# Dots with the experts of the last 14 first keys as one dense product of all prompt tokens, in a decoder step with product-key experts

## The reference, cut to what matters

```python
q = einsum('nd,de->ne', xf, w_q).reshape(N, 8, 2, 128)          # 8 heads, two half queries
sc = einsum('nhpc,pkc->nhpk', q, sub_keys)                      # 128 first keys, 128 second keys
s_top, i_top = top_k(sc, 16)
c_top, c_idx = top_k(all 256 sums of a first and a second, 16)
experts = e1 * 128 + e2                                         # 8 x 16 = 128 experts a token
gates = softmax(c_top)
h = einsum('nd,nkd->nk', xt, u_tab[experts])                    # dots with gathered rows of u
a = gates * gelu(h)
y = einsum('nk,nkd->nd', a, v_tab[experts])
```

## Time and profile before

| | us |
|---|---|
| median of 3 runs | 2494.46 (2492.43 to 2494.79) |
| profiled execution, its own time | 2485.81 |
| its span, first to last instruction | 2483.7 |
| PE busy | 1895.3 (76%) |
| DVE busy | 1708.6 (69%) |
| POOL busy | 1109.0 (45%) |
| ACT busy | 976.6 (39%) |
| mean transfer rate | 356 GB/s |

### The profile page before, as it was taken

The page is one execution under the profiler, slowest core; times in us unless marked ns, Lnnn a source line. Parts: engine busy times, 40 slices in busy tenths (PEclk is TensorE's granted clock), DMA queues, the critical chain, the costliest instruction groups (busy, mean ns, idle before and its releaser), DMA issues.

```text
span 2483.7 us, 27261 instructions
## 1 busy us (share of the span) xinstructions
PE 1895.3 (76%) x10395; PEld 1566.3 (63%) x10395; DVE 1708.6 (69%) x2335; ACT 976.6 (39%) x1603; POOL 1109.0 (45%) x484
## 2 busy tenths in 40 slices
PE   6998899899979745344233331999999999999798
PEld 5875778788769625343133231777777777777676
DVE  1056232422157988878899999899898988987723
ACT  3223122223223211111399992544444444444332
POOL 3663233345536346777676886122221222221154
PEclk9998899999989977667655555999999999999899
DMA  9997999988889879999999999899998999998547
GB/s 342 381 391 271 374 420 416 410 352 313 321 315 362 293 289 395 376 421 421 421 371 388 422 417 385 322 391 380 378 371 336 370 352 379 357 371 296 211 186 262
DMA packets 131808, 883.58 MB, mean 356 GB/s; under 512 B 19010, under 2 KB 20610, under 8 KB 55588
## 3 DMA queue, kind: packets, MB, share of 16 engines
q1 hardware_dynamic: 76388, 479.23, 50.7%
q0 software_dynamic: 55296, 402.68, 40.6%
HBM read 871.28 MB, written 141.63 MB: 408 GB/s over the span
## 4 chain that ended last, share of the span: by engine, by line
issue 28%; PE 25%; DMA 17%; DVE 14%; POOL 13%; ACT 2%; POOLq 0%; SPq 0%; ACTq 0%; DVEq 0%
DMA v_raw<-in_peer_v 9%; PE psum L1544 7%; PE psum L1546 7%; PE psum L1545 7%; POOL w_lo L553 6%; DMA expert_rows<-in_peer_u,experts 6%; POOL expert_rows L583 6%; DVE expert_rows L1355 5%; DVE v_lo L1486 2%; DVE x_tokens L1430 2%; DVE expert_rows L1421 2%; DMA ansposed_expert_rows<-in_peer_u,experts 1%; ACT v_hi L896 1%; PE psum L1891 1%; DMA ple_tokens<-in_p_sample 1%
## 5 line engine op out<-in xcount | busy, mean ns | idle before, releaser
L553 POOL TENSOR_TENSOR w_lo<-w_raw,w_hi 128x2048 fp32r<-128x2048 f32 x80 | 374.5, 4682 | 458.1 <-ACT w_hi L614 458.1
L583 POOL DMA_INDIRECT expert_rows<-in_peer_u,experts x238 | 466.1, 1958 | 186.8 <-DVE expert_rows L1355 117.1
L1544 PE MATMUL psum<-v_hi,gate_matrix_hi 128*128 128x512 f32 x1024 | 406.9, 397 | 38.9 <-DVE v_lo L1486 38.6
L896 ACT ACTIVATE v_hi<-v_raw 128x1024 fp32r<-128x1024 f32 x256 | 271.4, 1061 | 408.3 <-DMA v_raw<-in_peer_v 320.1
L1355 DVE SCALAR_TENSOR_TENSOR expert_rows<-expert_rows,x_tokens 128x2048 f32<-128x2048 f32 x174 | 393.4, 2289 | 45.6 <-DMA expert_rows<-in_peer_u,experts 43.3
L1545 PE MATMUL psum<-v_lo,gate_matrix_hi 128*128 128x512 f32 x1024 | 400.2, 391 | 0.0
L1546 PE MATMUL psum<-v_hi,gate_matrix_lo 128*128 128x512 f32 x1024 | 400.1, 391 | 0.0
L1486 DVE TENSOR_TENSOR v_lo<-v_raw,v_hi 128x1024 fp32r<-128x1024 f32 x256 | 310.1, 1220 | 85.0 <-ACT v_hi L896 84.4
L614 ACT ACTIVATE w_hi<-w_raw 128x2048 fp32r<-128x2048 f32 x80 | 153.2, 1915 | 374.4 <-PE psum L1546 285.0
L1544 PEld LDWEIGHTS psum<-v_hi,gate_matrix_hi 128*128 128x128 f32 x1024 | 192.8, 188 | 104.9 <-issue 40.2
L1846 PE MATMUL psum<-one_hot_first_gated,one_hot_second 128*128 128x128 f32 x448 | 107.7, 417 | 170.7 <-ACT one_hot_first_gated L800 167.5
(11 more groups left out here) (339 smaller groups left out, 3523.4 us busy)
## 6 DMA issues: line engine op xcount, KB each, us to landing
v_raw<-in_peer_v SPq DMA_DIRECT2D x256, 512.0 KB, 7.3
out<-in_state_attn_k SPq DMA_DIRECT2D x64, 1020.0 KB, 10.9
out<-in_state_attn_v SPq DMA_DIRECT2D x64, 1020.0 KB, 10.5
w_raw<-in_w_in SPq DMA_DIRECT2D x48, 1024.0 KB, 8.4
cache_part<-in_k_parts SPq DMA_DIRECT2D x40, 1024.0 KB, 10.5
cache_part<-in_v_parts SPq DMA_DIRECT2D x40, 1024.0 KB, 13.0
w_raw<-in_w_out SPq DMA_DIRECT2D x16, 1024.0 KB, 7.2
w_raw<-in_peer_wq SPq DMA_DIRECT2D x16, 1024.0 KB, 6.1
```

The lines of the kernel that those rows point to most:

```text
L553: nc.gpsimd.tensor_tensor(l_, r_, h_.bitcast(f32), ALU.subtract).then_inc(w_lo_ready, 1)
L583: pool.indirect_dma_start(ring[slot_of(n)][:, :], None, u_tab, bass.IndirectOffsetOnAxis(idx_p[:, t - 1, j:j + 1], 0)).then_inc(u_in[slot_ ...
L896: A(vhi[m % HS][:, :], vrl[m % RL][:, :], ACT.Copy).then_inc(vh_ok, 1)
L1544: MM(out, lh, rh, start=start, stop=False)
```

## The change

- `peer_u_T` is a further input: for each of the 14 first keys 114 to 127 the block of 128 rows of `u`, transposed to [128, 16, 128] (1 MB), laid out on the host.
- SP loads these blocks to two slots (`ut`) once the embedding output is written; PE multiplies each with all 256 prompt tokens (`block_product`: 16 products of 128 x 128 by 256 columns), block i - 1 behind PE row i. ACT applies gelu (`gelu_product`), and SP writes the results, [128 second keys, 14, 256 tokens], to the tensor `gelu_tab` in DRAM, in two parts behind the last load.
- `tokT` holds both halves' tokens. Their transposes (eight quarters, the second half's in pieces of 64 rows from two tiles) and copies stand behind the embedding product.
- The prompt's gathers get `bounds_check=KEPT`: a row index above 128 x 114 - 1 isn't gathered, and the slot keeps what it held. Three slots are zeroed once by POOL (three memsets, behind `lows(0, 66)`).
- `clear_dense` sets the dots of such pairs to 0, and `weigh` adds 1 to the gelu of 0, so that `gm` holds the plain gate there (`dense_pairs` makes the two masks).
- In the v stage, for k from 114, SP loads `gelu_tab[:, k]` (128 KB) to one of three slots ahead of piece 2k; DVE multiplies it by `gm[:, :, k]` behind piece 2k - 3 (`gate_times_gelu`), and the high and low parts are made from the product.
- `pe_dot(i)` stands behind the vector row with j = 6i + 10 (at most 109) of the first half's list.
- The builds wait for the gelus: ACT for `h_out`, PE for `h_ok`.

The diff, cut to its core:

```diff
+KD, KS = 14, 8
+K0 = NK - KD
+KEPT = K0 * 128 - 1
+PE_DOT_AT = {min(6 * i + 10, 109): i for i in range(len(PE_ROWS))}
...
+            sp.wait_ge(ple_out, 32)
+            for i in range(KD):
+                if i >= 2:
+                    sp.wait_ge(hd_mm, i - 1)
+                sp.dma_start(ut[i % 2][:, :, :].rearrange("p c s -> p (c s)"), peer_u_T[i]).then_inc(ut_in[i % 2], 16)
+            sp.wait_ge(h_ok, KS)
+            sp.dma_start(gelu_tab[:, 0:KS, :], gelu_a[:, :, :]).then_inc(h_out, 16)
+            sp.wait_ge(h_ok, KD)
+            sp.dma_start(gelu_tab[:, KS:KD, :], gelu_b[:, :, :]).then_inc(h_out, 16)
...
                 if m >= RL:
                     sp.wait_ge(vd_used, m - RL + 1)
+                if m == 2 * K0:
+                    sp.wait_ge(h_out, 32)
+                if m % 2 == 0 and m >= 2 * K0:
+                    i = m // 2 - K0
+                    if i >= 3:
+                        sp.wait_ge(al_ok, K0 + i - 2)
+                    sp.dma_start(gbuf[:, i % 3, :], gelu_tab[:, i, :]).then_inc(gk_in[i % 3], 16)
                 sp.dma_start(vrl[m % RL][:, :], v_rows[:, m // 2, m % 2, :]).then_inc(v_raw[m % RL], 16)
...
-            lows(0, 80)
+            lows(0, 66)
+            pool.wait_ge(w_used, 64)
+            for i in range(DSLOT, NSLOT):
+                nc.gpsimd.memset(ring[i][:, :], 0.0).then_inc(ring_set, 1)
+            lows(66, 14)
...
                 pool.indirect_dma_start(ring[slot_of(n)][:, :], None, u_tab,
-                                        bass.IndirectOffsetOnAxis(idx_p[:, t - 1, j:j + 1], 0)).then_inc(u_in[slot_of(n)], 16)
+                                        bass.IndirectOffsetOnAxis(idx_p[:, t - 1, j:j + 1], 0),
+                                        bounds_check=KEPT, oob_is_err=False).then_inc(u_in[slot_of(n)], 16)
...
+            def gelu_product(i):
+                if i == 0:
+                    act.wait_ge(ple_out, 32)
+                act.wait_ge(hd_mm, i + 1)
+                A(gelu_a[:, i, :] if i < KS else gelu_b[:, i - KS, :], PS[:, 6 + i % 2, 0:256], ACT.Gelu).then_inc(h_ok, 1)
...
-            act.wait_ge(ple_out, 32)
+            act.wait_ge(h_out, 32)
             one_hots(0)
...
-                    A(ghs[:, k % ST, :], gm[:, :, k], ACT.Copy).then_inc(ah_ok, 1)
+                    if k >= K0:
+                        act.wait_ge(gk_ok, k - K0 + 1)
+                    A(ghs[:, k % ST, :], weights_of(k), ACT.Copy).then_inc(ah_ok, 1)
...
+            def dense_pairs(t):
+                V.tensor_scalar(is_dense[:, t - 1, :], idx_p[:, t - 1, :], float(KEPT), None, ALU.is_gt)
+                V.memset(zeros[:, :], 0.0)
+                link(V.tensor_scalar(dense_f[:, t - 1, :], idx_p[:, t - 1, :], float(KEPT), None, ALU.is_gt))
+            def clear_dense(t, c0, w):
+                V.copy_predicated(hdot[:, t, c0:c0 + w], is_dense[:, t - 1, c0:c0 + w], zeros[:, 0:w])
...
+                if t > 0:
+                    link(V.tensor_tensor(hdot[:, t, c0:c0 + w], hdot[:, t, c0:c0 + w], dense_f[:, t - 1, c0:c0 + w], ALU.add))
...
-                    if t == 1 and j % 6 == 0 and 1 <= j // 6 <= NPE:
-                        pe_dot(j // 6 - 1)
+                    if t == 1 and j in PE_DOT_AT:
+                        pe_dot(PE_DOT_AT[j])
...
+            def gate_times_gelu(k):
+                i = k - K0
+                dve.wait_ge(gk_in[i % 3], 16 * (i // 3 + 1))
+                V.tensor_tensor(gbuf[:, i % 3, :], gm[:, :, k], gbuf[:, i % 3, :], ALU.mult).then_inc(gk_ok, 1)
...
                 V.tensor_tensor(vlo[m % RL][:, :], vrl[m % RL][:, :],
                                 vhi[m % HS][:, :].bitcast(f32), ALU.subtract).then_inc(vl_d, 1)
+                if m % 2 == 1 and (m + 3) // 2 in range(K0, NK):
+                    gate_times_gelu((m + 3) // 2)
                 if m in DECODE_AT:
                     decode_op(DECODE_AT[m])
...
+            def block_product(i):
+                pe.wait_ge(ut_in[i % 2], 16 * (i // 2 + 1))
+                if i >= 2:
+                    pe.wait_ge(h_ok, i - 1)
+                for f in range(KT):
+                    m = MM(PS[:, 6 + i % 2, 0:256], ut[i % 2][:, f, :], tokT[:, f, :], start=(f == 0), stop=(f == KT - 1))
+                m.then_inc(hd_mm, 1)
...
+                if 1 <= i <= KD:
+                    block_product(i - 1)
```

More of the change, by code:

```diff
@@ L155, in decoder_step @@
     rowT = at("expert_rows_T", [128, KT, 128], f32, 176 * KB)
-    tokT = at("prompt_tokens_T", [128, KT, 128], f32, 64 * KB)
+    tokT = at("prompt_tokens_T", [128, KT, 2 * 128], f32, 0)
+    ut = [at(f"expert_block_T{i}", [128, KT, 128], f32, (16 + 8 * i) * KB) for i in range(2)]
+    gelu_a = at("gelu_products_first", [128, KS, 2 * 128], f32, 32 * KB)
+    gelu_b = at("gelu_products_last", [128, KD - KS, 2 * 128], f32, 64 * KB)
     xb = at("second_half_tokens", [128, D], f32, 120 * KB)
@@ L301, in decoder_step @@
         ab_mm, ev_a = sem("gate_matrix_psum"), sem("gate_matrix_act")
-        act_step = sem("act_step")
+        act_step, ring_set = sem("act_step"), sem("row_slots_set")
+        ut_in = [sem("expert_block_slot0_in"), sem("expert_block_slot1_in")]
+        hd_mm, h_ok, h_out = sem("block_products"), sem("gelu_products_ready"), sem("gelu_products_written")
+        gk_in, gk_ok = [sem(f"gelu_of_key_slot{i}_in") for i in range(3)], sem("gate_times_gelu")
         x_sc, x_acc = sem("x_scaled"), sem("x_in_sums")
@@ L838, in _ @@
                 ple_copy(n)
+            row_T_copies(-2)
+            row_T_copies(-1)
             for i in range(NPE):
                 row_T_copies(i)
+                if 1 <= i <= KD:
+                    gelu_product(i - 1)
                 if i == 1:
@@ L1394, in _ @@
                     prompt_dot(*row)
-                    if t == 1 and j % 6 == 0 and 1 <= j // 6 <= NPE:
-                        pe_dot(j // 6 - 1)
+                    if t == 1 and j in PE_DOT_AT:
+                        pe_dot(PE_DOT_AT[j])
+                    if j == (40, 12)[t - 1]:
+                        dense_pairs(t)
+                    if t == 2 and j == 15:
+                        dve.wait_ge(h_out, 32)
                     if j in after_dot[t]:
@@ L1868, in row_block_dot @@
                     f = 4 * q + j
-                    m = MM(PS[:, 2 + i % 2, 0:128], rowT[:, f, :], tokT[:, f, :], start=(f == 0), stop=(f == KT - 1))
+                    m = MM(PS[:, 2 + i % 2, 0:128], rowT[:, f, :], tokT[:, f, 0:128], start=(f == 0), stop=(f == KT - 1))
                 if q == 3:
                     m.then_inc(pd_mm, 1)
-            for q in range(4):
-                row_block_T(-1, q)
+            def block_product(i):
[5 more added lines that the diff above has]
+                m.then_inc(hd_mm, 1)
             pe.wait_ge(ple_in, 48)
@@ L1894, in _ @@
             pe.wait_ge(ple_ok, 12)
+            pe.wait_ge(xb_in, 32)
+            for i in (-2, -1):
+                for q in range(4):
+                    row_block_T(i, q)
             for i in range(NPE):
                 if i == 0:
-                    pe.wait_ge(pt_ok, 4)
+                    pe.wait_ge(pt_ok, 8)
                 row_block_T(i, 0)
@@ L2047, in cache_parts, with blocks_T @@
         return ("k_parts", k_parts.reshape(NB * PARTS, 128, -1)), ("v_parts", v_parts.reshape(NB * PARTS, 128, -1))
+    def blocks_T(u):
+        u = _np.asarray(u).reshape(NK, 128, KT, 128)[K0:]
+        return u.transpose(0, 3, 2, 1).reshape(KD, 128, -1)
     for name in _INS:
@@ L2053 @@
         give(f"in_{name}", pieces(inputs[name]) if name in ("w_in", "w_out", "peer_wq", "ple_gate") else inputs[name])
+        if name == "peer_u":
+            give("in_peer_u_T", blocks_T(inputs[name]))
     cos, sin = _rope_tables()
```

41 lines of the change are left out of this document (29 added, 12 removed).

## The result

The changed kernel takes 2508.1 us (median of 15 runs, 2495.8 to 2522.2); the kernel before, run beside it, 2491.5 (15 runs, 2484.6 to 2502.6). The ratio is 1.0075, 95% interval 1.006 to 1.009: 0.75% or 19 us slower (the two medians alone stand 16.6 us apart). The forecast was 2509. The profiled execution took 2510.9 us, with a span of 2509.1.

The account below looks back on a forecast made before the run. Row stage: transfer bytes set the pace in about 400 us, DVE in the rest; then the v stage, with PE leading in part. A to F sum 2 - 4 + 9 - 9 + 2 + 15 = +15 on 2494.5: 2509 us, range 2477 to 2538.

Parts of the forecast that it names:

- F: V stage, last 14 keys: gelu row issued only in its own piece, so DVE and PE wait; +15 us (+3 to +30).
- C: Row stage, first half: block loads and gelu writes added, skipped rows saved; +9 us (+3 to +25).
- A: Three POOL memsets beside the layer norm on the path; +2 us (0 to 8).
- B: Start of row stage: DVE's first PE-dot wait goes, but token transposes delay row 0; -4 us (-8 to +2).
- D: Row stage, second half: no blocks, skipped rows save from 1350 us on; -9 us (-14 to -3).
- E: Twelve small DVE operations (compares, memsets, predicated copies, additions), 3.4 us, partly where DVE waits anyway; +2 us (1 to 3.4).
- L: V stage, last 14 keys: landing time of a gelu row after issue, 6.9 us for four keys, 3.1 to 3.8 for ten.
- rival 1: V stage: the gelu row is there when DVE comes to it; F and the sum are +3, 2497 us; chance 0.17.
- rival 3: First half: PE becomes the bound if the granted clock stays at 0.68; +27 more, 2536 us; chance 0.08.
- Rival 2: Row stage: the gathers' own queue, not bytes, sets 2.48 us; blocks ride free, sum -16, 2478 us; chance 0.15.

Follow-up runs that it names:

- second profile: The changed kernel and the kernel before, each profiled once more unchanged: 2514.2 and 2482.1 us, one run each.
- experiment 1: Changed kernel with each key's gelu row issued one key (two pieces) earlier on the SP queue: 2492.1 us, ratio 1.0010 to the kernel before.
- experiment 5: Kernel before with only the new place of the PE dots, behind the vector row j = 6i + 10: 2480.7 us, ratio 0.9977.
- experiment 6: Changed kernel with the PE dots read back behind vector row 6(i + 1): 2515.3 us, ratio 1.0121 to the kernel before.
- experiment 4: Changed kernel with the bounds taken off the prompt's gathers, so all rows are fetched: 2536.5 us, ratio 1.0186 to the kernel before.
- experiment 3: Also called skips alone: changed kernel without dense blocks, their products, the table and its v-stage product; gathers still skip: 2468.9 us, ratio 0.9918 to before.
- experiment 7: Changed kernel with two block loads in place of 14, all 14 block products kept: 2483.2 us, ratio 0.9995 to the kernel before.

## Why the prediction was right, and where not

Its sum was +15; the runs give +19 (0.75%), and most of it, +16, is term F, the one it named as the largest. That the rest came out near is in part luck, as C was 6.6 us too small while A and B were 5.1 us too unfavourable. The terms, as the difference of the profiles shows them:

| term | forecast | profiles |
|---|---|---|
| A memsets | +2 | 0 |
| B start | -4 | -7.1 (to -3.7) |
| C first half | +9 | +15.6 |
| D second half | -9 | -7.5 |
| F last 14 keys | +15 | +10.4 (+17.4 in the second profile) |
| E, and the rest | +2 | +1 |

The first profile's terms come to +12.2; the other 13.1 us of its longer span lie ahead of the first dot (below). The twelve DVE operations of E are busy for 2.6 us in it (3.4 forecast); what they cost in time is inside C and D, and "the rest" is what lies outside the stages named.

**A.** The three memsets lie beside the layer norm, and none of its DVE products became longer. Timelines of POOL and DVE, changed kernel:

```profile
715.09 5.29 POOL L597 MEMSET expert_rows<- 128x2048 f32 x3
...
721.02 2.35 DVE L1259 SCALAR_TENSOR_TENSOR x_tokens<-x_tokens,ln_mean_var,ln_gain_bias 128x2048 f32<-128x2048 f32 x1
```

2.35 us; its like in the kernel before, at 708.14 with no POOL instruction beside it, took 2.35 too. The norm product ahead of it took 6.47 us from 710.83, beside the subtraction and then for 2.2 us beside the memsets, and its like before took 6.46. The memsets end at 720.4, just ahead of 721.02, so the trace shows no product fully beside one; it shows that they delay none here. The Trainium skill's rule (SBUF — State Buffer, Who interferes with whom), by which this term is 0, is not contradicted.

**B.** The first PE dot no longer waits. The added token transposes do stand ahead of row 0: its own transposes start 6.7 us behind the embedding product, where it was 0.7 (6.0 us more, with 7 forecast). But this product started 14.6 us ahead of the first dot, and in the kernel before 7.0. So row 0 is ready when it was, and POOL waits for it as long as before:

```profile
867.36 23.82 PE L1976 MATMUL psum<-ple_weights,ple_T 128*64 128x512 f32 x48 [0.47 <-ACT ple_T L851]
...
904.20 0.99 POOL L608 DMA_INDIRECT ansposed_expert_rows<-in_peer_u,experts  x1 [10.26 <-PE psum L1940]
```

10.26 us, as the 10.24 of the earlier trace rows, 22 us after the first dot in both; DVE lacked a row for 0.83 us there. So the whole wait was gained, where the forecast took half, and in part by chance. Over the twelve profiles the embedding product starts at 858.8 to 867.4 us while the first dot lies between 868.8 and 881.9, so the two don't move together. In experiment 1, which has the change's code there, it started 10.8 us ahead of the first dot, POOL waited 13.77 us, and dot 14 stands at -4.6 in place of -7.1. Experiment 5 gives 6 us, experiment 6 a row stage 4.5 longer.

**C, the step that failed.** From dot 14 to dot 110 the change loses 15.6 us. Four kernels take it apart (experiments 5, 4 and 3, and the change); each number is the second table's difference between the two dots. The one with neither blocks nor skips, experiment 5, also lacks the masks, the memsets and the second half's token transposes:

| | without blocks | with blocks |
|---|---|---|
| all rows gathered | +1.4 | +33.7 |
| rows skipped | -11.5 | +15.6 |

With the blocks there the skips give 18.1 us, 15.9 of them from dot 33 on (forecast 11 + 5 = 16). The late part was right as well: from dot 33 on the change loses 5.9 us, where 20 + 4 - 16 = +8 was forecast. The mis-sized number is "six fall before 1000, in the stretch with share 0.86, and cost me +1". Seven loads had in fact landed by 1003 us, two of them before dot 14. By dot 33 (1009 us) the change has lost 9.8 us since dot 14, with the other five. Skips alone had gained 2.2 there, so the early blocks cost 12.0. Experiment 7, with all of PE's products but no load between these dots, loses 0.2: 9.6 of the 12.0 are the five loads, 1.9 each of the 2.5 that a load's bytes take at 420 GB/s, and 2.4 are the rest. The step took a mean share of 0.86 over 114 us, 16 us of room, for room that six loads (15 us) would find. Shorter windows of the kernel before show what the mean is made of:

```profile
887.00:907.00 20.00, 11.56 (x97) 10.84 (x96) 14.54 (x56) 5.50 (x9) 7.60 (x6) 0.88 0.99 372
907.00:927.00 20.00, 0.00 (x0) 0.00 (x0) 19.68 (x27) 0.00 (x0) 10.15 (x6) 0.50 0.61 223
927.00:947.00 20.00, 14.22 (x101) 13.51 (x102) 15.09 (x18) 6.19 (x12) 14.50 (x9) 0.77 0.97 388
947.00:967.00 20.00, 8.57 (x58) 8.14 (x58) 16.26 (x18) 2.43 (x5) 17.26 (x10) 0.66 1.01 425
967.00:987.00 20.00, 10.37 (x74) 9.94 (x73) 19.12 (x58) 3.58 (x6) 11.03 (x6) 0.74 1.01 421
...
950.00:1000.00 50.00, 16.73 (x108) 15.69 (x107) 45.92 (x95) 4.94 (x9) 29.40 (x16) 0.67 0.85 350
```

The transfers are full (0.97 to 1.01) except for two holes, 907 to 927 and behind 987 (0.61 in 987 to 1007), both behind or beside a DVE selection, in which no dot frees a slot. A block's load isn't tied to a hole: from the third on it is issued when PE has used its slot, here at 926.4, 955.1, 967.9, 980.9 and 993.7 us, each the end of a block's products:

```profile
L530 SPq DMA_DIRECT2D expert_block_T<-in_peer_u_T x14: 327/328/433, 906.4 to 1136.2; - x14
...
DMA to landing us min/median/max: 8.8/9.6/14.4
```

In the change the stretch has share 0.91 over 118 us, so 10.6 us of room are left and only some 5 were taken (an estimate from two stretches that don't hold quite the same work); the other 10 of the 15 us went to the dots' account, which is what the table has. From 950 to 1000 the share is now 1.00, and DVE is busy 33.9 us where it had 45.9.

A second reading of the four kernels: skips are worth 13.0 us without blocks, where DVE is busy 181 of 210 us, and 18.1 with them, where it is busy 166. That DVE's own pace caps the first is a likely reason and was not tried. An edit's worth depends on its company. Over both halves blocks and skips cancel: 14 x 1.05 + 1.84 = 16.5 MB come in and cost 27.2 us, 1.6 us per MB; 28.5 MB go out and give 18.1 + 7.5 us, 0.9 per MB.

**D.** From dot 110 to the last the change gains 7.5 us, of it 0.4 up to dot 174 and the rest behind: 9 was forecast. The view of the dots' line from 1350 on, with the last 64 of them and what DVE waited for:

```profile
L1407 DVE SCALAR_TENSOR_TENSOR expert_rows<-expert_rows,second_half_tokens x64: 2283/2292/2294, 1404.2 to 1554.9; 128x2048 f32<-128x2048 f32 x64
...
  DMA expert_rows<-in_peer_u,experts: 6.2, 26
```

The 64 start 150.7 / 63 = 2.39 us apart, within the 2.3 to 2.4 named as the sign; the waits were 12.1 us in 57, and the share is 0.96 for 0.99.

**F.** The mechanism is the one forecast. Timeline of DVE, at the first key and at the one behind the norm weights, and the timeline of SP at the latter:

```profile
2247.29 0.58 DVE L1507 TENSOR_TENSOR gelu_of_key<-gate_matrix,gelu_of_key 128x256 f32<-128x256 f32 x1 [4.02 <-DMA gelu_of_key<-gelu_products]
...
2304.36 0.60 DVE L1507 TENSOR_TENSOR gelu_of_key<-gate_matrix,gelu_of_key 128x256 f32<-128x256 f32 x1 [9.14 <-DMA gelu_of_key<-gelu_products]
```

```profile
2291.12 2.27 SPq L562 DMA_DIRECT2D ln_gain_bias<-in_ln_b  x1
2293.43 0.43 SPq L557 DMA_DIRECT2D v_raw<-in_peer_v  x1
2295.61 0.33 SPq L556 DMA_DIRECT2D gelu_of_key<-gelu_products  x1
```

The row of piece 244 is issued at 2295.61 and DVE gets it at 2304.36, 8.7 us later, the longest landing of the 14. The shortest is 2.0 and the median 3.9: the forecast's L (6.9 for four keys, 3.1 to 3.8 for ten; the 3.1 stands in no row) was of the right size, though a row of 128 KB can land faster than any v piece did. The DVE waits of 29.8 us became 10 to 17 us of v stage, as PE covers part of each. Timed, F is 16 us (1.0075 against 1.0010), forecast 15; the 2 us of it that were priced for the products don't show. All twelve profiles agree: the v stage takes 760.3, 767.3, 769.2, 774.1 and 764.0 us in the five executions with the late row (the change twice, experiments 4, 6 and 7), and 743.9 to 753.2 in the seven without it. The Trainium skill (DMA: Bandwidth & Descriptors, Queues, rings and completion order) says that the write that reports a transfer done lands only after every earlier write of that engine across its queues. The trace is in keeping with it, the longest landing, 8.7 us for 128 KB, being the one behind the norm weights, but it can't tell this from plain queueing. By the figures of the Trainium skill (DMA: Bandwidth & Descriptors, Measured) that rival 1 weighs, the row would have been in time; the measured landings decide against it.

**PE and ACT** cost little, where nothing was forecast: at most the 6.9 us of experiment 7 that are not told apart. A block takes 7.1 us:

```profile
947.99 7.07 PE L1958 MATMUL psum<-prompt_tokens_T,expert_block_T 128*128 128x256 f32 x32
```

7.8 had been forecast. The granted clock rose to 0.83 to 0.89 ("near 1" only in 950 to 1000, at 0.97), so **rival 3's** condition (a clock left at 0.68) never came, and experiment 7, with all of PE's work, is 20 us faster than the change. **Rival 1** is experiment 1: not what the change does, but what it would do with the row in time, 2492 us, no change in time, as that rival's price had it (+3). **Rival 2** (the gather queue and not the bytes) would have had gathers 2.2 us apart with the blocks beside them and nothing lost to them; in the change they are issued 2.55 us apart between 1009 and 1220, and experiment 7 shows that the block loads cost the dots time.

**What stays open.** The first dot comes 9 to 13 us later in the changed kernel's first profile than in those of before, but it comes at 870.2 to 880.3 in the experiments that hold the change's code ahead of it, and at 868.8 to 875.3 in the three profiles without it; the POOL subtraction before the memsets already starts 12.9 us later than its like in the earlier trace rows, where no edit has come yet. It is a spread between executions, and a share of a few us that the change may have in it can't be told from it. The timed sum doesn't need one: 1 (row stage, against the first profile of before; 5 against the second), 16 (F) and 1 (the rest) are 18 to 22, and 19 were measured.

## What to carry to other kernels

A mean transfer share below 1 is no free room: cut the stretch into short windows (20 us here), find the holes, and ask whether the new load is issued in one; if its issue hangs on something else, it can cost most of its time (1.9 of 2.5 us here). A small load whose user comes straight after it is to be issued earlier; here three changed lines, two pieces earlier, were worth 16 us. And an edit that comes along in a larger change is to be timed alone: the new place of the PE dots, on the kernel before and with nothing else, has the lowest ratio of all that compute everything (0.9977).

## What the hardware showed that was not expected

- A gather with rows skipped keeps all its packets (55,296) and the engines stay busy (0.99) at a lower rate, 391 GB/s in place of 420: 10.6% of the prompt's row bytes gave 4.4 to 4.7% of the time between dots 57 and 110 in skips alone. Part of that may be DVE's own pace, so how much of a packet's time a skipped row keeps was not settled.
- The POOL instruction of a gather took 0.99 us with bounds, where the one of the earlier trace rows took 0.94.
- Reading the weights of a key from a dense slot and not with the stride of `gm` makes their low part 0.42 us in place of the 0.61 of the earlier trace rows. For ACT's high part it is 0.40 in place of 0.66. On DVE that is 2.7 us over 14 keys, about a third of what the products with the gelu row add (14 x 0.61 = 8.5). It may be one reason why the products cost nothing; that was not tried alone.
